# LN1's rows loaded over two x1 tiles, three pairs of expert weight buffers, a ring of four row buffers

## The reference

```
x1  = layernorm(ALPHA * x + mix)                  # LN1, gain and bias of 1024
e1, e2 = two experts of 32 for each token          # group first, then top 2 inside it
y   = sum over e in (e1, e2): gate_e * (silu(x1 @ Wg_e) * (x1 @ Wu_e)) @ Wd_e
out = layernorm(ALPHA * x1 + y)                    # LN2
```

## Time and profile before

| | us |
|---|---|
| runs before (3) | 599.1 median, 598.02 to 601.4 |
| the profiled execution | 599.66 |
| its span, first to last instruction | 598.0 |
| PE busy | 519.1 (87%) |
| DVE busy | 372.9 (62%) |
| ACT busy | 190.9 (32%) |
| POOL busy | 134.7 (23%) |
| mean granted TensorE clock | 0.981 |
| chain that ended last: PE | 60% of the span |
| chain that ended last: DMA | 23%, of it arena_o<-in_w_gu 19% |

### The profile page before, as it was taken

The page is one execution under the profiler, slowest core; times in us unless marked ns, Lnnn a source line. Parts: engine busy times, 40 slices in busy tenths (PEclk is TensorE's granted clock), DMA queues, the critical chain, the costliest instruction groups (busy, mean ns, idle before and its releaser), DMA issues.

```text
span 598.0 us, 8961 instructions
## 1 busy us (share of the span) xinstructions
PE 519.1 (87%) x3296; PEld 280.1 (47%) x3296; DVE 372.9 (62%) x722; ACT 190.9 (32%) x356; POOL 134.7 (23%) x156
## 2 busy tenths in 40 slices
PE   6999999999988978999999798888887867867860
PEld 5887788874355533455456643333332222222220
DVE  0652059898935585643177766678885667666686
ACT  0100384213345552141132122444443334432340
POOL 1001054600028730000000202333323231221231
PEclk9999999999999999999899999999998989999996
DMA  8950008570709631003967599999999999999951
GB/s 308 379 178 6 1 1 348 212 256 1 282 3 361 272 145 56 2 35 137 424 225 304 190 417 412 405 394 418 416 416 409 421 415 418 416 414 418 403 205 41
DMA packets 34298, 157.95 MB, mean 264 GB/s; under 512 B 12712, under 2 KB 12712, under 8 KB 20304
## 3 DMA queue, kind: packets, MB, share of 16 engines
q1 hardware_dynamic: 20880, 127.46, 53.2%
q0 software_dynamic: 10752, 29.59, 13.1%
q10 hardware_dynamic: 2624, 0.34, 0.4%
HBM read 160.12 MB, written 21.23 MB: 303 GB/s over the span
## 4 chain that ended last, share of the span: by engine, by line
PE 60%; DMA 23%; ACT 7%; DVE 6%; issue 3%; SPq 1%; POOL 0%; POOLq 0%; ACTq 0%; DVEq 0%
DMA arena_o<-in_w_gu 19%; PE ps L496 17%; PE ps L970 11%; PE ps L756 9%; PE ps L993 4%; PE ps L597 3%; PE ps L659 2%; PE ps L643 2%; ACT arena_s L1253 2%; PE ps L680 2%; PE ps L955 1%; DMA x_rows<-arena_s 1%; PE ps L563 1%; PE ps L819 1%; DMA arena_s<-first_rows,known 1%
## 5 line engine op out<-in xcount | busy, mean ns | idle before, releaser
L970 PE MATMUL ps<-arena_w,arena_s 128*64 128x512 f32 x368 | 110.9, 606 | 22.3 <-DMA arena_o<-in_w_gu 10.9
L496 PE MATMUL ps<-arena_w 128*128 128x260 f32 x416 | 95.0, 389 | 5.2 <-DMA arena_w<-in_xT 4.7
L496 PEld LDWEIGHTS ps<-arena_w 128*128 128x128 f32 x416 | 79.8, 193 | 19.9 <-DMA arena_w<-in_xT 5.4
L970 PEld LDWEIGHTS ps<-arena_w,arena_s 128*64 128x64 f32 x368 | 33.5, 139 | 96.3 <-issue 68.8
L993 PE MATMUL ps<-arena_w,cs 128*64 128x512 f32 x184 | 54.8, 599 | 20.8 <-ACT cs L1269 20.8
L756 PE MATMUL ps<-arena_o,arena_s 128*128 128x512 f32 x128 | 61.6, 629 | 1.6 <-DVE arena_s L1614 1.6
L970 PE MATMUL ps<-arena_o,arena_s 128*64 128x512 f32 x112 | 53.6, 629 | 0.0
L1486 DVE STREAM_TRANSPOSE arena_s<-arena_w 128x1024 f32<-128x1024 f32 x36 | 42.0, 1215 | 8.3 <-PE ps L597 8.2
L2163 POOL DMA_INDIRECT first_rows<-arena_s,known x15 | 18.0, 1202 | 113.7 <-ACT arena_s L1276 104.8
L1923 DVE TENSOR_TENSOR arena_s<-arena_s,ps 128x256 f32<-128x256 f32 x16 | 6.7, 420 | 55.8 <-ACT arena_s L1265 55.8
L756 PEld LDWEIGHTS ps<-arena_o,arena_s 128*128 128x128 f32 x128 | 24.5, 201 | 33.4 <-issue 33.3
(11 more groups left out here) (349 smaller groups left out, 893.1 us busy)
## 6 DMA issues: line engine op xcount, KB each, us to landing
arena_w<-in_w_gu SPq DMA_DIRECT2D x46, 1024.0 KB, 20.1
arena_w<-in_w_dn SPq DMA_DIRECT2D x23, 1024.0 KB, 20.2
arena_o<-in_w_gu SPq DMA_DIRECT2D x14, 1024.0 KB, 23.4
arena_o<-in_w_dn SPq DMA_DIRECT2D x7, 1024.0 KB, 23.8
arena_w<-in_w_in SPq DMA_DIRECT2D x12, 512.0 KB, 13.1
arena_o<-in_w_out SPq DMA_DIRECT2D x1, 4096.0 KB, 13.8
arena_s<-in_w_gu SPq DMA_DIRECT2D x4, 1024.0 KB, 8.1
first_rows<-in_x_tok SPq DMA_DIRECT2D x1, 2080.0 KB, 18.5
```

The costliest lines, as they stand in the source:

```text
L496: last = mm(ps[rows, b + n, 0:HALF], lhs(k), rhs(k)[:, n * HALF:(n + 1) * HALF], start=(k == 0), stop=(k == ks - 1))
L970: last = mm(ps[64 * e:64 * e + 64, 2 + q, :], xgT[:, k, CAP * e:CAP * (e + 1)], gu_w[2 * slots + e][:, k, :], start=(k == 0), stop=(k == K ...
```

## The change

The diff, cut to what moves instructions or buffers:

```
-S_YB, S_LNG = 7168, 3 * D
+S_YB, S_LNG = 7168, 0
-S_XG = [5120, 6144, 0, D, S_RT] + [S_SLOT + D * n for n in range(3)]
-S_YO = [S_SLOT + 3 * D, 2 * D, S_SLOT + 4 * D]
+S_XG = [5120, 6144, 3 * D, 4 * D]
+S_YO = [S_RT, 2 * D]
+BUFFER = (0, 1, 2, 0, 1, 0, 1, 2)
+def pair_buffer(n):
+    return n if n < HEAD else BUFFER[(n - HEAD) % BODY]
...
             for t in range(TT):
+                if t == TT - 1:
+                    sp.wait_ge(tile_cleared, 1)
                 sp.dma_start(x1[0:ROWS[t], t, :], x_tok[...]).then_inc(xtok_landed, 16)
...
             store_x1(3)
+            landed(sp, x1_stored, 4)
+            sp.wait_ge(x1T_ps, 2)
+            sp.dma_start(lng, lns[0:2].partition_broadcast(P)).then_inc(ln1_landed, 16)
             sp.wait_ge(o_done, 16)
             for half in range(2):
                 gate_up(3, slice(3, 4), half)
             down(3, slice(3, 4))
             store_x1(4)
+            gate_up(4, slice(4, 5), 0)
             landed(sp, x1_stored, TT)
             landed(sp, gathered[0])
-            for half in range(2):
-                gate_up(4, slice(4, 5), half)
+            gate_up(4, slice(4, 5), 1)
             down(4, slice(4, 5))
-            sp.dma_start(lng, lns[0:2].partition_broadcast(P)).then_inc(ln1_landed, 16)
             sp.dma_start(lng2, lns[2:4].partition_broadcast(P)).then_inc(ln1_landed, 16)
...
-            with sp.Fori(0, n_rounds * (NE // 4) - 3) as it:
-                refill(0, (it * 4 + 10) % NE, it * 2 + 4)
-                refill(1, (it * 4 + 12) % NE, it * 2 + 5)
-            refill(0, NE - 2, past + (NPAIR - 2))
+            with sp.Fori(0, n_rounds * 2 - 1) as it:
+                for n in range(HEAD + 2, HEAD + 2 + BODY):
+                    refill(it, n)
+            for n in range(HEAD + 2 + BODY, NPAIR):
+                refill((past,), n)
...   ScalarE, in each step
-                root(it, n - 2)
+                root(it, n - 1)
...   DVE
-                stt(x, x, ALPHA, lng[:, 0, :], ALU.mult, ALU.mult).then_inc(residual_step, 1)
+                stt(x, x, ROW_MAX, lng[:, 0, :], ALU.min, ALU.mult).then_inc(residual_step, 1)
...
-                stt(x, x, stat[:, 2:3], lng2[:, 1, :], ALU.mult, ALU.add).then_inc(out_ready, 1)
+                stt(yo[n % 2], x, stat[:, 2:3], lng2[:, 1, :], ALU.mult, ALU.add).then_inc(out_ready, 1)
...
                 residual(it, n + 1)
                 if n == 1:
                     own_part(it, 0)
-                if n >= 2:
-                    finish(it, n - 2)
+                if n >= 1:
+                    finish(it, n - 1)
                 own_part(it, n)
...
             landed(dve, ln1_landed, 3)
+            link(ts(lng[:, :, :], lng[:, :, :], ALPHA, None, ALU.mult))
...   POOL
+            pool.wait_ge(s_done, 4 * NH)
+            G.memset(x1[:, TT - 1, :], 0.0).then_inc(tile_cleared, 1)
...
                 scatter_own(it, n)
-                if n >= 2:
-                    scatter_out(it, n - 2)
                 if n >= 1:
-                    gather_other(it, n)
-                if n == 1:
-                    pool.wait_ge(dn_ps, HEAD)
-                gather_rows(n + 4, ...)
+                    scatter_out(it, n - 1)
+                    gather_rows(n + 3, ...)
+                    gather_other(it, n)
```

More of the change, by code:

```diff
@@ L120, in nth, with before_in, weights_landed @@
     return v if it is None else it * (BODY // per * by) + v
+def pair_buffer(n):
+    return n if n < HEAD else BUFFER[(n - HEAD) % BODY]
+def before_in(n):
+    d = 1
+    while BUFFER[(n - HEAD - d) % BODY] != pair_buffer(n):
+        d += 1
+    return d
+def weights_landed(it, n):
+    if n < HEAD:
+        return 32
+    m, q = n - HEAD, pair_buffer(n)
+    per = BUFFER.count(q)
+    v = 32 * (2 + m // BODY * per + BUFFER[:m % BODY].count(q))
+    return it[0] * (4 * per) + v if isinstance(it, tuple) else it * (32 * per) + v
 def hymba_step(nc, xT, x_tok, kv_cache, rope_cache, conv_st, rec_st, page_rep, lane, w_in, w_kpe, w_uq, w_uk,
@@ L338, in ring @@
         def ring(n):
-            return n % BODY
-        def other(it, n):
-            return 2 if isinstance(it, tuple) and n == NPAIR - 1 else n % 2
+            return n % 4
         def landed(eng, s, n=1):
@@ L443, in _, with refill @@
             store_x1(4)
+            gate_up(4, slice(4, 5), 0)
             landed(sp, x1_stored, TT)
             landed(sp, gathered[0])
[L446 to L447 removed]
+            gate_up(4, slice(4, 5), 1)
             down(4, slice(4, 5))
[L449 removed]
             sp.dma_start(lng2, lns[2:4].partition_broadcast(P)).then_inc(ln1_landed, 16)
[L451 removed]
+            def refill(it, n):
+                q, used = pair_buffer(n), nth(it, n, add=1 - before_in(n))
+                e = 2 * n if it is None or isinstance(it, tuple) else (it * (2 * BODY) + 2 * n) % NE
                 for half, done in enumerate((gu_half, gu_ps)):
                     sp.wait_ge(done, used)
[L455 to L456 removed]
+                    for j in range(2):
+                        gate_up(2 * q + j, slice(e + j, e + j + 1) if isinstance(e, int) else bass.ds(e + j, 1), half)
                 sp.wait_ge(dn_ps, used)
[L458 to L461, removed]
+                for j in range(2):
+                    down(2 * q + j, slice(e + j, e + j + 1) if isinstance(e, int) else bass.ds(e + j, 1))
+            refill(None, HEAD)
+            refill(None, HEAD + 1)
             sp.wait_ge(routed, 1)
@@ L977, in products @@
                     turn_tokens(it, n + 1)
+                else:
+                    for _ in range(5):
+                        mm(ps[:, 7, 0:P], ident[:, :], ident[:, :], start=True, stop=True)
                 return slots, landed_count
@@ L1994, in _ @@
                 pair_step((past,), n)
-            finish((past,), NPAIR - 3)
+            finish((past,), NPAIR - 2)
             hidden((past,), NPAIR - 1)
-            finish((past,), NPAIR - 2)
-            own_part((past,), NPAIR - 1, True)
-            finish((past,), NPAIR - 1)
+            finish((past,), NPAIR - 1, True)
         @block.gpsimd
@@ L2228, in _ @@
                 pair_step((past,), n)
-            n = NPAIR - 1
-            gather_other((past,), n)
-            for k in range(3):
-                scatter_out((past,), n - 2 + k)
-            fixed()
-            landed(pool, out_landed, n_rounds * NPAIR)
+            gather_other((past,), NPAIR - 1)
+            scatter_out((past,), NPAIR - 2)
+            ready, before, stored = number(nth((past,), NPAIR - 1, add=1), nth((past,), NPAIR - 1, 1, 16), n_rounds * (16 * NPAIR))
+            scatter_out((past,), NPAIR - 1, ready, before)
+            pool.wait_ge(out_landed, stored)
 def _lay_out(i):
```

87 lines of the change are left out of this document (45 added, 42 removed).

## The result

| | before | after |
|---|---|---|
| median us (4 runs each, same chip) | 599.81 | 646.82 |
| profiled execution, its span | 599.66, 598.0 | 646.88, 645.0 |
| PE busy, us | 519.1 | 537.4 |
| mean granted TensorE clock | 0.981 | 0.928 |

The ratio is 1.0796, 95% interval 1.0760 to 1.0831 (the two medians alone give 1.0784): slower by 47 us.

What follows compares the result with a forecast made beforehand. A per-pair loop through finish and other gather was taken to set the pace: 374.1 + 3 + 218.4 + 2 x 12.1 + 10.6 = 630.3, then 634.8 at the span's end, 636 us as measured; range 608 to 653.

Steps and rivals of the forecast that it cites:

- main forecast: Whole kernel: slower, 628 to 645 us, with the point at 636; chance 0.58.
- rival C: Other gather's latency under weights is 13.9 us, so 23.2 a loaded turn and 647 us in all; chance 0.13.
- The loop: Once per pair: finish n-1, output scatter, x1 gather, other gather, finish n; 9.3 us plus the other gather's latency.
- X: Time from the other gather's issue to its landing, third in POOL's queue; taken as 10.5 us under weights, 4.1 unloaded.
- The count of loaded turns: Turns 1 to 12: nine under weights at 19.8 us and three without at 13.4, together 218 us.
- Start of the loop: First finish on DVE ends at 374.1 us, plus 3 for loads that delay the first pair; alpha multiplication costs nothing.
- after 341: Sign of a right forecast: TensorE's first transposes of pair 0 come after 341 us.
- Turns 13 and 14: Turns near the end without x1 gather or weights: 12.1 us each.
- Last pair: From hidden 15 through down products, addition and rest of the finish: 10.6 us, of which 5.0 to the down products' end.
- The edits costed at nothing: Third buffer, waits on out_landed, clearing of tile 4 and the LN1 alpha multiplication: 0 us each.
- Rival A: Turns settle where the DMA is just full: 16.7 us each, 618 us in all, or about 624; chance 0.20.
- Rival B: Loop stays hidden behind TensorE or DMA, earlier loads take 5.0 us off: 594.6, or 597 us; chance 0.07.

Runs made afterwards that it cites:

- e1: Changed kernel with POOL issuing the other gather of n ahead of the output scatter of n-1; 606.04 us, ratio 1.0111 to the kernel before.
- e2: Changed kernel with the other gather behind the output scatter of n-1 but ahead of the x1 gather; 633.05 us.
- e3: Changed kernel with seven eighths of the bytes of every weight refill left out, instructions and order kept; 582.67 us.
- e11: e10 with the LN1 rows and all of slot 4 loaded where the kernel before loads them, and 8 fewer idle-time TensorE products; 599.09 us.
- e7: e1 with 8 more idle-time TensorE products before the first gather and hidden of pair 15 ahead of the finish of pair 14; 598.63 us.
- e8: e1 with the LN1 rows and all of slot 4 loaded behind the first gather, third buffer kept; 605.36 us, ratio 1.0124 to the kernel before.
- e10: e7 with POOL's order of the changed kernel in step 1 alone; 599.84 us, ratio 1.0020 to the kernel before.
- e4: Kernel before with only the earlier loads (LN1 rows, half of slot 4) and the last x1 tile cleared; 601.98 us, ratio 1.0042.
- e12: e10 with all of slot 4 behind the first gather and 8 fewer idle-time TensorE products, LN1 rows still early; 600.15 us.
- e6: e1 with two pairs of weight buffers in turn from pair 3 on; 610.42 us, ratio 1.0202 to the kernel before.

## Why the prediction was right

The 646.8 us lie in the stated range (608 to 653), but 2 us above the main forecast of 628 to 645, in the stretch between it and rival C. What was right is the mechanism; the terms were off as follows.

- **The loop** is as it was said, with each of its steps: own terms 21.06 - 11.59 = 9.5 us in the mean of eight loaded turns (9.3 predicted). e1, e2 and e3 each break or shorten another part of it and move the time: by 41 us where it is broken, 14 where a loaded turn is 3.3 us shorter (1.3 of issue, 2.0 of latency), 64 where the gather is unloaded. (The prediction's heading calls the finish one step later; its text has it right, n-1 in step n instead of n-2.)
- **X** was taken as 10.5; the loaded gathers took 10.7 to 12.5, mean 11.6 (start to addition; one of 6.7 lay half in a gap). The row from the third place, 11.4, was the better guide than the middle, though that gather moves twice the bytes; e2 shows that the place in the queue counts, and whether the bytes of the gather count at all was not tried. A loaded turn was 21.1 instead of 19.8.
- **The count of loaded turns** came from bytes: nine and three were predicted, eight, one of 16.0 and three of 13.2 to 13.7 came. Twelve turns took 224.9 us (378.83 to 603.73), 218.4 predicted. With nine at the measured 21.1 it would have been 230, so the count, which was too high by one, took back some 5 us of the error in X.
- **Start of the loop:** the first finish ended at 377.9 (377.1 predicted). The size was right, a part of its cause wasn't seen: the first x1 gather went out 0.9 us later (336.41), and behind the longer pause the granted clock was 0.50 from 344 to 347. The first transposes came at 340.80, just short of the "after 341" that was to show it.
- **Turns 13 and 14:** 12.6 and 11.6, together 24.2; 12.1 each was predicted, so the two misses of 0.5 cancel. **Last pair:** 13.4 instead of 10.6. The term that was off is the 5.0 us from hidden 15 to the end of the down products: it was 7.8 (627.01 to 634.81), of which the down products took 6.2 and not the 3.65 of the earlier trace rows. That row holds at a granted clock of 1.00; here the finish of pair 14 ahead of hidden 15 gave TensorE a pause of 8.09 us, and the clock stood at 0.50 behind it.
- The sum: 646.9 - 636 = 10.9 us missed, of which 6.5 are turns, 2.8 the last pair, 0.8 the start, the rest small.
- **The edits costed at nothing** leave no trace of much more: the first finish ended 0.8 us late with the alpha multiplication, the clearing and a slower first pair in it, and POOL's waits for a landed output scatter ahead of the other gather come to 1.1 us. In e1 the wait on out_landed does appear (POOL 18.3 us), since there the loop no longer hides it.
- **Rival A** (turns of 16.7) was seen in one turn of twelve. **Rival B** (the loop stays hidden) didn't come: the other gather landed 3.5 us after its issue at least and 12.1 at most, and from start to addition it took under 5 only where the weights had a gap (95, 161 and 134 GB/s under the three such gathers of the first twelve turns) or were through. The rule of the Trainium skill, page "DMA: Bandwidth & Descriptors", section "Anatomy of one DMA — SWDGE (gpsimd) path", gives an estimated 2.3 us for this gather. With seven eighths of the refills' bytes gone (e3) it is 2.9 to 4.6, near that; under the stream of weights the trace doesn't agree. **Rival C** had the time, 647, and half of the reason: X above 10.5, but 11.6 and not 13.9.

What stays open: how long a gather takes that overlaps the end of the backlog (one took 6.7 us) was not tried, nor whether a third `yo` buffer would take the last 18 us of POOL's waits out of e1.

## What to carry to other kernels

Where a small gather's result is needed in the same step as it is issued, its latency behind a saturated stream of weights is part of the step: put it ahead of whatever waits for the consumer, or keep a step between. Loads that were moved into an early hole paid nothing here, because the DMA engines ran dry elsewhere instead; look for that place before you move them. And an order that makes TensorE pause just before the last products can make them dearer: 1.06 us each for 0.59 here.

## What the runs showed of the hardware

- One other gather (128 slots, of which a quarter hold a row of 4 KB: 520 tokens over 16 pairs) landed 2.9 to 4.6 us from issue in e3, where the DMA engines were a third busy (96 GB/s from 380 to 550 us). Under the weights it took 9.6 us behind one scatter (e2) and 11.6 behind a scatter and another gather (changed kernel), both the mean from start to addition. So the one gather ahead cost 2.0 us beside its issue of 1.3.
- The granted clock behind TensorE's pause before the first transposes: 1.00 throughout 340 to 350 us where the pause was 0.20 us (e11), 0.81 (e7), 0.85 (before) and 0.92 (e8); 0.50 in a part of it where the pause was 1.42 (e10), 1.71 (changed kernel), 2.24 (e4), 2.38 (e12), 3.21 (e6) and 3.92 (e1). e10 has the idle-time products of e7, but they ended at 338.4 us there and at 340.3 in e7, and its clock was 0.66 over 340 to 350.
